# A gate unit streamed through the first attention instead of after it

## What is computed

```
xn = rmsnorm(x);  q_lat, kv_lat, k_rope, dq, dk, dv, gate_pre = split(xn @ w_in)
o_mla  = causal_attention(8 heads: q, k of 64+32 dims from the latents, v of 64)
dq, dk = rope(dq), rope(dk)                       # 4 heads x 2 x 64 dims
o_diff = rmsnorm(attn(dq1, dk1, dv) - lam * attn(dq2, dk2, dv))
gates  = sigmoid(gate_pre + b_gate)               # 2 x 1024 columns
merged = gates[:, :1024] * (o_mla @ w_branch_mla) + gates[:, 1024:] * (o_diff @ w_branch_diff)
x      = x + merged @ w_out                       # then the feed-forward, then the second block
```

## Time and profile before

| | |
|---|---|
| median of 3 runs | 1318.38 us (1318.19 to 1318.41) |
| the profiled execution, by its own time | 1318.19 us |
| its span in the trace | 1316.3 us |
| PE busy | 1281.3 us (97%) |
| DVE busy | 691.5 us (53%) |
| ACT busy | 536.2 us (41%) |
| POOL busy | 56.9 us (4%) |
| chain that ended last | PE 91%, DVE 5%, ACT 2%, issue 1%, POOL 1% |

### The profile page before, as it was taken

One profiled execution on the slowest core, in us unless ns is written; L12 is line 12 of the kernel. 1 busy time (PEld: TensorE's weight loads), 2 busy tenths in 40 slices (PEclk: granted clock), 3 DMA queues, 4 the chain that ended last, 5 costly groups with the idle time before them and its releaser, 6 DMA issues.

```text
span 1316.3 us, 15811 instructions
## 1 busy us (share of the span) xinstructions
PE 1281.3 (97%) x6226; PEld 1068.2 (81%) x6226; DVE 691.5 (53%) x1044; ACT 536.2 (41%) x903; POOL 56.9 (4%) x97
## 2 busy tenths in 40 slices
PE   8999999999999999999999989999999999999997
PEld 6877778877888888888888868888988888888885
DVE  6775877644555444444443257745543435435554
ACT  5545655652334343434323143426554334223222
POOL 0001331211000000000000000000000000000000
PEclk9999999999999999999999989999999999999999
DMA  5232112122432333223223322431114333232221
GB/s 193 68 96 65 33 44 69 50 64 67 171 115 80 111 96 96 96 96 112 96 80 97 111 64 88 120 96 33 33 33 144 97 96 96 96 96 97 92 84 64
DMA packets 104427, 116.39 MB, mean 88 GB/s; under 512 B 13422, under 2 KB 88236, under 8 KB 104364
## 3 DMA queue, kind: packets, MB, share of 16 engines
q1 hardware_dynamic: 104240, 115.49, 27.8%
q10 hardware_dynamic: 124, 0.03, 0.0%
HBM read 113.42 MB, written 2.10 MB: 88 GB/s over the span
## 4 chain that ended last, share of the span: by engine, by line
PE 91%; DVE 5%; ACT 2%; issue 1%; POOL 1%; DVEq 0%; ACTq 0%; POOLq 0%
PE ps_mm L1867 58%; PE ps_mm L1902 20%; PE ps_o L2243 2%; PE ps_o L2054 1%; PE ps_s L2031 1%; DVE w_lo L1121 1%; PE ps_t L2223 1%; PE ps_mm L1873 1%; PE ps_mm L1962 1%; ACT w_hi L619 1%; PE ps_t L2041 1%; PE ps_s L2075 1%; ACT tmp L644 1%; PE ps_o L2097 1%; PE ps_s L2208 1%
## 5 line engine op out<-in xcount | busy, mean ns | idle before, releaser
L1867 PE MATMUL ps_mm<-act_hi,w_hi 128*128 128x512 f32 x944 | 372.5, 395 | 2.6 <-DVE w_lo L1130 1.5
L1867 PE MATMUL ps_mm<-act_lo,w_hi 128*128 128x512 f32 x944 | 370.6, 393 | 0.0
L1867 PE MATMUL ps_mm<-act_hi,w_lo 128*128 128x512 f32 x944 | 370.3, 392 | 0.0
L1121 DVE TENSOR_TENSOR w_lo<-stage,w_hi 128x2048 fp32r<-128x2048 f32 (+3 forms) x77 | 156.7, 2035 | 197.7 <-ACT w_hi L619 197.5
L1867 PEld LDWEIGHTS ps_mm<-act_hi,w_hi 128*128 128x128 f32 x944 | 177.7, 188 | 39.0 <-DVE w_lo L1121 2.3
L1867 PEld LDWEIGHTS ps_mm<-act_hi,w_lo 128*128 128x128 f32 x944 | 177.5, 188 | 35.3
L1867 PEld LDWEIGHTS ps_mm<-act_lo,w_hi 128*128 128x128 f32 x944 | 177.6, 188 | 34.5
L619 ACT ACTIVATE w_hi<-stage 128x2048 fp32r<-128x2048 f32 (+3 forms) x78 | 133.2, 1708 | 174.7 <-PE ps_mm L1902 127.5
L1534 DVE TENSOR_TENSOR w_lo<-stage,w_hi 128x2048 fp32r<-128x2048 f32 x23 | 52.7, 2293 | 56.3 <-ACT w_hi L905 56.2
L1902 PE MATMUL ps_mm<-w_hi,act_hi 128*128 128x512 f32 x176 | 68.6, 390 | 0.0
L1902 PE MATMUL ps_mm<-w_hi,act_lo 128*128 128x512 f32 x176 | 68.5, 389 | 0.0
(11 more groups left out here) (382 smaller groups left out, 1971.9 us busy)
## 6 DMA issues: line engine op xcount, KB each, us to landing
stage<-in_w_in SPq DMA_DIRECT2D x44, 1024.0 KB, 5.3
stage<-in_w_ffn_gate SPq DMA_DIRECT2D x11, 1024.0 KB, 5.4
stage<-in_w_ffn_up SPq DMA_DIRECT2D x11, 1024.0 KB, 5.3
stage<-in_w_ffn_down SPq DMA_DIRECT2D x10, 1024.0 KB, 5.1
stage<-in_w_out SPq DMA_DIRECT2D x4, 1024.0 KB, 5.0
stage<-in_w_att_out SPq DMA_DIRECT2D x4, 1024.0 KB, 5.0
stage<-in_w_sg_out SPq DMA_DIRECT2D x4, 1024.0 KB, 5.0
stage<-in_w_o SPq DMA_DIRECT2D x4, 1024.0 KB, 4.9
```

Of the source, the lines that this page charges most:

```text
L1121: V.tensor_tensor(w_lo[:, s, 0:k * w], stage[:, s, 0:k * w], w_hi[:, s, 0:k * w].bitcast(F32), ALU.subtract).then_inc(w_lo_made, 1)
L1867: ins = T.matmul(ps_mm[:, 2 * bank_slot + m, :], wt[:, kk, m * P:(m + 1) * P], acts[ap][:, kk, :], start=(r == 0), stop=(r == per - 1), sk ...
```

## The change

The stream of the first attention gets a fifth unit, 15, with 48 more matmuls. Its weights become equal: 4 for each of the steps 3 to 31, where they had been 5, 4, 2, 4 by p % 4 (2 for the steps with 384 keys). What doesn't fit into the 35 steps is done after the last one as a last piece (weight 6). The gates of unit 15 are kept in `dq[:, 0:2, :]` in the place of `gates[:, 0:2, :]`; DVE's `gate_norm` of them waits for the last queries (`qd_lo_made`), and SP waits for `merged_lo` of the first two merged tiles before it loads the residual over them.

```diff
-MLA_STREAM = Stream(U0["dk"], [48] * 4, [0, 0, 2] + [(5, 4, 2, 4)[p % 4] for p in range(3, 4 * MH)] + [5] * LAG)
+
+MLA_STREAM = Stream(U0["dk"], [48] * 5, [0, 0, 2] + [4] * (4 * MH - 3) + [5] * LAG + [6])
```

```diff
+        def gate_tile(c):
+
+            return dq[:, c, :] if c < 2 else (gates, gates_b)[c // 8][:, c % 8, :]
```

```diff
             sp.wait_ge(diff_pv_done, 4 * DH)
+            sp.wait_ge(merged_lo, 2)
             for t in range(TT):
                 sp.dma_start(res[:, t, :], xv[:, t, :]).then_inc(res_landed, 16)
```

On ACT:

```diff
                 for u, m in MLA_STREAM.banks.get(p, ()):
-                    diff_bank(u, m)
+                    if u == U0["gate_m"]:
+                        gate_bank(u, m, m)
+                    else:
+                        diff_bank(u, m)
                 for u, m in MLA_STREAM.banks.get(p - 2, ()):
-                    if u >= U0["dq"]:
+                    if U0["dq"] <= u < U0["gate_m"]:
                         diff_q_hi(2 * (u - U0["dq"]) + m)
...
-                if p == MLA_STEPS + 1:
-                    hi(U0["gate_m"] + 1)
-            for m in range(2):
-                gate_bank(U0["gate_m"], m, m)
```

On DVE:

```diff
                 for u, m in MLA_STREAM.banks.get(p, ()):
                     n = 2 * (u - U0["dk"]) + m
+                    if u == U0["gate_m"]:
+                        dve.wait_ge(qd_lo_made, 2 * DH)
+                        gate_norm(u, m, m)
+                        continue
                     dve.wait_ge(bank_free_act, act_freed(group_of(u), m))
...
-                if p == MLA_STEPS + 1:
-                    lo(U0["gate_m"] + 1)
...
-            for m in range(2):
-                gate_norm(U0["gate_m"], m, m)
```

On PE:

```diff
                     ins.then_inc(pv_done, 1)
-            straight(U0["gate_m"], "F", acts_x)
+            stream(MLA_STREAM, MLA_STEPS, lambda u: acts_x)
```

More of the change, by code:

```diff
@@ L656, in gate_bank @@
             def gate_bank(u, m, c):
-                g = (gates, gates_b)[c // 8][:, c % 8, :]
+                g = gate_tile(c)
                 act.wait_ge(bank_free, freed(u, m))
@@ L888, in merge_hi @@
                 act.wait_ge(merged, c + 1)
-                nc.scalar.activation(mg_hi[:, c, :], gates[:, c, :], ACT.Copy, scale=0.5).then_inc(merged_hi, 1)
+                nc.scalar.activation(mg_hi[:, c, :], gate_tile(c), ACT.Copy, scale=0.5).then_inc(merged_hi, 1)
             for i in range(1, 4):
@@ L1373, in diff_q_lo, with gate_norm @@
                                     ALU.subtract).then_inc(qd_lo_made, 1)
+            def gate_norm(u, m, c):
+                V.tensor_tensor(gate_tile(c), bank(u, m), xr_b[:, :], ALU.mult
+                                ).then_inc(bank_free, 1)
             def diff_k_lo(hd, piece):
@@ L1424, in _ @@
                         lo_half(u + 1, h)
-                if p == MLA_STEPS + 1:
-                    lo(U0["gate_m"] + 1)
-            def gate_norm(u, m, c):
-                V.tensor_tensor((gates, gates_b)[c // 8][:, c % 8, :], bank(u, m), xr_b[:, :], ALU.mult
-                                ).then_inc(bank_free, 1)
             def gated(u, m, c):
                 dve.wait_ge(gates_made, c + 1)
-                g = (gates, gates_b)[c // 8][:, c % 8, :]
+                g = gate_tile(c)
                 V.scalar_tensor_tensor(out=g, in0=g, scalar=1.0, in1=bank(u, m),
                                        op0=ALU.add, op1=ALU.mult).then_inc(bank_free, 1)
-            for m in range(2):
-                gate_norm(U0["gate_m"], m, m)
             dve.wait_ge(lam_exp, 1)
@@ L1499, in merge @@
                 dve.wait_ge(bank_free, freed(u, m))
-                V.tensor_tensor(gates[:, c, :], gates[:, c, :], gates_b[:, c, :], ALU.add).then_inc(merged, 1)
+                V.tensor_tensor(gate_tile(c), gate_tile(c), gate_tile(8 + c), ALU.add).then_inc(merged, 1)
             def merge_lo(c):
                 dve.wait_ge(merged_hi, c + 1)
-                V.scalar_tensor_tensor(out=mg_lo[:, c, :], in0=gates[:, c, :], scalar=0.5,
+                V.scalar_tensor_tensor(out=mg_lo[:, c, :], in0=gate_tile(c), scalar=0.5,
                                        in1=mg_hi[:, c, :].bitcast(F32), op0=ALU.mult, op1=ALU.subtract
```

## The result

| | before | after |
|---|---|---|
| median | 1318.38 us (5 runs, 1317.76 to 1320.12) | 1323.54 us (5 runs, 1322.16 to 1324.44) |
| profiled execution, its own time | 1318.19 us | 1322.16 us |
| its span | 1316.3 us | 1320.4 us |
| waits of PE in the first attention and at the entry into the second | 5.8 us | 8.9 us |

A forecast was written before the change was run, and what follows sets the result against it. PE, busy 97% of the span, was taken as the bound, so only its waits could change: loop 8.2 plus entry 1.2 minus 5.7 gave +3.7 us on 1318.19, 1322.0 as median, range 1318.0 to 1325.0.

The forecast's parts named there:

- The winnable part, 5.7: Loop of the first attention: 5.7 us of PE waits before the change, the most that could be won.
- The lengths of the steps: Loop steps with 7 matmuls and no wait: 2.58, 3.11, 3.77, 2.95 us for 128, 256, 384, 512 keys.
- 0.38: Steps with 384 keys before the change: value product starts 0.38 us after the stream matmul, 0.15 of it wait.
- The collision: Steps 13, 20, 27: rope starts beside key piece and w_lo half, delaying DVE; loop waits 8.2 us against 5.7.
- 29 and 30: Late loop steps: the pile of step 27 makes PE wait 1.2 and 0.75 us, before 0 and 0.15.
- 27: Loop step 27: queries, key piece and w_lo half in step 26 make PE wait 1.4 us, before 1.35.
- The rival in which DVE keeps its turn: Loop: the w_lo half behind the key piece goes before POOL; 1318.2 us, no change, chance 0.25.
- The entry: Start of the differential attention: PE's scores of differential step 1 wait 1.2 us, before 0.
- The clock's rival: Steps 22 and 23, 29 and 30: PE's clock falls at both pairs of waits, +3.4, 1325.4 us, chance 0.08.
- Costs taken as nothing: SP's new wait, DVE's wait for qd_lo_made and ACT's tanh among exponentials: no time added.
- om_lo beside a rope: Step 7 after the change: om_lo beside POOL's rope could lose 0 to 1.08 us; taken as 0.
- The sum: Whole kernel: 8.2 + 1.2 - 5.7 = +3.7 us on 1318.19, so 1321.9, or 1322.0 as median.

The follow-up runs named there:

- pieces_apart: The changed kernel with the key pieces of heads 0 to 2 moved to steps where no w_lo half stands behind them: 1314.99 us, ratio to before 0.9978.
- short_ropes: The changed kernel with the rotary embedding of the differential keys and queries left out but for 8 of 512 columns: 1315.42 us in one time.
- write_only_ropes_long: The changed kernel with each tile's rope operations replaced by seven memsets, so POOL runs as long but only writes: 1315.96 us in one time.
- equal_shares_alone: The kernel before with equal shares for its four units, the gate unit still after the loop: 1317.27 us, ratio to before 0.9992.
- after_again: The changed kernel once more, unaltered, for its profile alone: 1320.98 us.

## Why the prediction was right

Forecast 1322.0 (1318.0 to 1325.0), slower at 0.53; measured 1323.5. The direction and the mechanism were right. That the number came so near is partly luck: the waits were forecast 0.6 us too high, and what the clock adds was not in the sum.

- **What bounds the kernel.** Right: nothing of PE's work changed, the difference is waits that start-to-start reading finds. The winnable part, 5.7, is 5.8 by the same reading of the whole list.
- **The lengths of the steps.** Right but for one. Without waits the steps with 128, 256 and 512 keys last 2.59, 3.12 and 2.98 us (forecast 2.58, 3.11, 2.95). Those with 384 keys last 3.66 with 7 matmuls, not 3.77. Where nothing waits, no 0.38 is left in them.
- **The collision.** Right in place and size; the table above has step by step what the walk gave. The largest errors are 29 and 30 (1.95 forecast, 1.41 measured) and 27 (1.4, 1.59). pieces_apart shows that it is the order, short_ropes and write_only_ropes_long that it is the rope's reads, for the long waits of the loop but that of step 27. In one point the text of the prediction was wrong: the scaling of the probabilities has one tensor as input and not two, and yet it was held up by POOL (last section).
- **The rival in which DVE keeps its turn** is out: in the steps 13, 20 and 27 POOL's waiting operation went before the w_lo half that stood next in DVE's queue (2.18 us at 163.55). Where the half comes right behind the shuffle it does go first, and that is what pieces_apart lives on.
- **The entry.** 1.2 forecast, 1.32 measured, by the chain that was forecast; two key pieces out of it took it away.
- **The clock's rival** is out in this stretch: PEclk is 1.00 in every stretch from 107 to 218 us of after, with waits of 0.84 and 1.87 in steps running and of 1.59 after them. The 0.81 of 98 to 107 us, from which the rival took its price, isn't a fixed cost of the waits there either: with the same two waits the clock in that stretch was 1.00 in seven of the fourteen traces, short_ropes and equal_shares_alone among them. The Trainium skill (TensorE: Matmul & The Clock Gate, A second HAM failure mode) describes a kernel in which TensorE idled for short times so often that its clock went up and down; in the stretch from 107 to 218 us this trace doesn't show it.
- **Costs taken as nothing.** The first load of the residual was issued at 344.6 us before and at 347.7 after, the last at 348.0 and 350.7: no later than the 3.1 us by which all is shifted, so `merged_lo` costs nothing. ACT's loads of its function tables are 22 in both traces. om_lo beside a rope: in step 7 of after it took 0.67 us from 118.95 on, with POOL at work from 117.47 to 119.59, while the scaling behind it took 1.42:

```profile
118.95 0.67 DVE L1408 TENSOR_TENSOR om_lo<-ps_o,om_hi 64x512 fp32r<-64x512 f32 x1
...
119.73 1.42 DVE L1416 TENSOR_SCALAR prob<-prob,small 128x384 f32<-128x384 f32 x1
```

- **The sum.** The waits came to 8.9 instead of 9.4, so +3.1 instead of +3.7 (and 3.7 on the median of 1318.38 is 1322.1, not 1322.0). PE's matmuls behind the wait of the pass between the blocks start 3.14 us later in the trace of after (784.89 against 781.75), which is what the waits explain. The other 0.9 us of the profiled execution's 3.97 come behind that point, where the clock was 0.80 over 25 us against 0.86. The median is 5.2 us longer, 2 more than the waits explain. Here the mean granted clock of each execution helps. All five of after had 0.992. Before had 0.992 in ten of the 57 executions that were timed beside the experiments, and those ten took 1320.24 to 1320.76 us; most others had 0.994 to 0.996. After's five took 1322.16 to 1324.44, median 1323.54: at the same clock it is about 3 us slower, as the waits say. So the 2 us go with the lower clock, though of before's own five executions only the profiled one's clock is on record (0.993). after_again, at 0.996 and 1320.98 us, shows that the changed kernel can have the higher clock too. Whether it has the lower one more often than before, or five times by chance, stays open.

## What to carry to other kernels

When work is streamed through a loop earlier, everything that is hung on the stream's progress moves too: here the weight splits and the ropes met a fixed table of key pieces, and a change of which PE's own arithmetic says -5.7 us gave +3 to +5. List what each queue gets in each step before and after, and look at the in-order queues of the engines that aren't busy: DVE is busy 53% of the time and still set every one of these waits. A copy that needs nothing late (pt) can be the thing PE waits for, because of what stands ahead of it.

## What the runs showed of the hardware

In these traces a DVE operation with both inputs in SBUF and a POOL operation that reads SBUF exclude each other for their whole length, and whoever has waited goes first, so they alternate: a key piece's 0.69 us became 1.78, POOL's 1.27 became 2.16. Beside POOL memsets, which only write, the same DVE operations keep their time (0.687 and 1.219 us mean); but the scaling of the probabilities, one input in SBUF and one output, does not: its mean for 512 columns was 0.49 us with short ropes, 0.64 beside long memsets and 0.80 beside whole ropes:

```profile
L1416 DVE TENSOR_SCALAR prob<-prob,small 128x512 f32<-128x512 f32 x8 | 3.9, 487 | 0.3
```

```profile
L1417 DVE TENSOR_SCALAR prob<-prob,small 128x512 f32<-128x512 f32 x8 | 5.1, 641 | 0.3
```

```profile
L1416 DVE TENSOR_SCALAR prob<-prob,small 128x512 f32<-128x512 f32 x8 | 6.4, 804 | 0.3
```

The Trainium skill (SBUF — State Buffer, Who interferes with whom) states both: two inputs in SBUF contend with POOL's reads only, and the two-port modes that tensor_scalar can enter with any POOL operation. The traces agree. No row names the mode, but undisturbed the scaling took 0.29, 0.35, 0.42 and 0.49 us for 128, 256, 384 and 512 columns, 0.07 per 128, where a two-input operation goes from 0.69 us for 512 columns to 1.22 for 1024, 0.13 per 128.
